# Hyena stage of a hybrid SSD/Hyena/MoE layer: first tap of the short convolution on ScalarE, and the projection halves added ahead of the lane's last remainder

## The reference

```python
u3 = short_conv(p[..., COL_HY:COL_GATE], hy_conv_w, hy_conv_b, rows)   # 3 taps, rows of 64 tokens, zero padding
v, x1, x2 = jnp.split(u3, 3, axis=-1)                                   # 3 x 2048 channels
z2 = x1 * fft_long_conv(v, kf[:, 0], hy_bias[0])
y_hy = x2 * fft_long_conv(z2, kf[:, 1], hy_bias[1])
merged = gates[..., :D] * (y_ssd @ w_ssd_out) + gates[..., D:] * (y_hy @ w_hy_out)
```

## Time and profile before

| | |
|---|---|
| median of 3 runs | 2260.49 us (2258.45 to 2261.85) |
| profiled execution, own time | 2255.41 us |
| its span | 2253.5 us |
| granted TensorE clock, mean | 0.981 |
| TensorE busy, share of span | 95% |
| VectorE / ScalarE / GpSimd busy | 70% / 46% / 5% |
| Hyena lanes 0 to 23 in the span | 734.7 to about 1128 us |

### The profile page before, as it was taken

The page is one execution under the profiler, slowest core; times in us unless marked ns, Lnnn a source line. Parts: engine busy times, 40 slices in busy tenths (PEclk is TensorE's granted clock), DMA queues, the critical chain, the costliest instruction groups (busy, mean ns, idle before and its releaser), DMA issues. The chain is left out here.

```text
span 2253.5 us, 30840 instructions
## 1 busy us (share of the span) xinstructions
PE 2141.1 (95%) x11866; PEld 1734.2 (77%) x11866; DVE 1587.6 (70%) x2195; ACT 1040.5 (46%) x1385; POOL 120.1 (5%) x143
## 2 busy tenths in 40 slices
PE   5999998999999999999999999998899999999997
PEld 2578886546899877777789999986688888778775
DVE  3357787766664678888876445556677777899998
ACT  4243233123654433333443434444655555677776
POOL 2000000000000002020210100000000000000000
PEclk9999999999999999999999999998999999999999
DMA  9954556887576635443434656733588888899995
GB/s 323 366 194 148 189 178 229 302 321 260 176 231 183 178 116 154 133 139 117 136 119 149 173 171 185 242 116 140 161 283 285 272 273 276 311 358 386 364 338 210
DMA packets 314047, 500.60 MB, mean 222 GB/s; under 512 B 16957, under 2 KB 160594, under 8 KB 312752
## 3 DMA queue, kind: packets, MB, share of 16 engines
q1 hardware_dynamic: 308672, 480.80, 64.3%
q0 software_dynamic: 5232, 17.86, 2.4%
HBM read 496.46 MB, written 2.13 MB: 221 GB/s over the span
## 5 line engine op out<-in xcount | busy, mean ns | idle before, releaser
L189 DVE TENSOR_TENSOR w_lo<-raw,w_hi 128x1024 fp32r<-128x1024 f32 x680 | 831.3, 1251 | 373.9 <-ACT w_hi L185 361.9
L185 ACT ACTIVATE w_hi<-raw 128x1024 fp32r<-128x1024 f32 x680 | 707.6, 1058 | 582.0 <-PE bank L197 450.9
L195 PE MATMUL bank<-h,w_hi 128*128 128x256 f32 (+1 forms) x896 | 294.8, 329 | 11.5 <-DVE w_lo L189 5.9
L197 PE MATMUL bank<-h,w_lo 128*128 128x256 f32 (+1 forms) x896 | 290.2, 324 | 0.0
L196 PE MATMUL bank<-h,w_hi 128*128 128x256 f32 (+1 forms) x896 | 290.2, 324 | 0.0
L1624 PE MATMUL bank<-h,w_hi 128*128 128x512 f32 x768 | 280.6, 408 | 4.6 <-DVE w_lo L189 4.6
L1626 PE MATMUL bank<-h,w_lo 128*128 128x256 f32 x768 | 217.9, 284 | 0.0
L195 PEld LDWEIGHTS bank<-h,w_hi 128*128 128x128 f32 x896 | 173.0, 193 | 38.6 <-issue 17.3
L1624 PEld LDWEIGHTS bank<-h,w_hi 128*128 128x128 f32 x768 | 147.3, 192 | 47.5 <-issue 12.3
L197 PEld LDWEIGHTS bank<-h,w_lo 128*128 128x128 f32 x896 | 172.8, 193 | 13.1
L196 PEld LDWEIGHTS bank<-h,w_hi 128*128 128x128 f32 x896 | 173.2, 193 | 12.4 <-issue 0.5
(11 more groups left out here) (498 smaller groups left out, 3684.2 us busy)
## 6 DMA issues: line engine op xcount, KB each, us to landing
raw<-in_w_in SPq DMA_DIRECT2D x240, 512.0 KB, 4.4
raw<-in_ada_w SPq DMA_DIRECT2D x192, 512.0 KB, 6.2
raw<-in_moe_w_gate SPq DMA_DIRECT2D x128, 512.0 KB, 5.2
raw<-in_moe_w_up SPq DMA_DIRECT2D x128, 512.0 KB, 5.6
raw<-in_moe_w_down SPq DMA_DIRECT2D x128, 512.0 KB, 6.0
raw<-in_w_ssd_out SPq DMA_DIRECT2D x32, 512.0 KB, 4.6
raw<-in_w_hy_out SPq DMA_DIRECT2D x32, 512.0 KB, 3.4
raw<-in_w_o SPq DMA_DIRECT2D x32, 512.0 KB, 3.8
```

The source lines that it names most:

```text
L185: act.activation(self.k.w_hi[:, j % HL, :], self.k.raw[:, j % RAW, :], ACT.Copy).then_inc(self.hi_ready, 1)
L189: dve.tensor_tensor(self.k.w_lo[:, j % HL, :], self.k.raw[:, j % RAW, :], self.k.w_hi[:, j % HL, :].bitcast(F32), ALU.subtract).then_inc(s ...
L195: pe.matmul(out, lhs[0], rhs[0], start=start, stop=False)
L197: return pe.matmul(out, lhs[1], rhs[0], start=False, stop=stop)
```

## The change

In lanes b = 1 to 24, for the channels of lane b-1:

- VectorE's `conv` is split. `halves(b-1)`, the two additions L1925, now stands between `split_lo` of q = 2 and of q = 3. The rest stays behind q = 3 (and, where pp is 5, behind `decayed`, `scaled` and `lows`, as before).
- The first tap (two instructions) goes to ScalarE as `first_tap(b-1)`: two `Identity` activations of 128 x 256 with per-channel scale and bias, right behind q3's `split_hi` and so ahead of the side work. It waits for `halves(b-1)`. For the four lanes with b % 6 == 4 the first tap stays on VectorE.
- `conv(b-1)` on VectorE then waits for the first tap and does the four instructions of taps two and three. The waits on `folded` (which keep v and x1 from being overwritten) go to ScalarE with the tap. The counts of `padded` become two per lane.

```diff
-                        pe.wait_ge(s.padded, b - 1)
+                        pe.wait_ge(s.padded, 24 + b - 1)
...
+                def first_tap(b):
+                    i, part, half = b // 6, b % 6 // 2, b % 2
+                    if b % 6 == 4:
+                        return
+                    act.wait_ge(s.summed, b + 1)
+                    if i and part == 0:
+                        act.wait_ge(s.folded, 2 * i - 1)
+                    if i and part == 1:
+                        act.wait_ge(s.folded, 2 * i)
+                    tile = i * 4 + part * KT + 2 * half
+                    for c in range(2):
+                        out = (v, x1, x2)[part][:, 2 * half + c, :].rearrange("p (r n) -> p r n", r=ROWS)
+                        tap = pad[:, c, :].rearrange("p (r n) -> p r n", r=ROWS)[:, :, LEAD:LEAD + GRID_W]
+                        w, bias = VEC_AT["hy_conv_w"] + tile + c, VEC_AT["hy_conv_b"] + tile + c
+                        ins = act.activation(out, tap, ACT.Identity, bias=k.vcol[:, bias:bias + 1],
+                                             scale=k.vcol[:, w:w + 1])
                     ins.then_inc(s.padded, 1)
...
                         st.split_hi(act, 0, 192, HY0 + 4 * b + 3)
+                        if 0 < b < 25:
+                            first_tap(b - 1)
                         if i and pp == 1:
                             keep_spectrum(first)
...
-                def conv(b):
-                    i, part, half = b // 6, b % 6 // 2, b % 2
-                    dve.wait_ge(s.padded, b + 1)
+                def halves(b):
+                    dve.wait_ge(s.padded, 2 * b + 1)
                     for c in range(2):
                         x = rows_of(pad[:, c, :])[:, :, 2:2 + GRID_W]
                         ins = dve.tensor_tensor(x, x, rows_of(k.psum[2 * (b % 2) + c][:, L:2 * L]), ALU.add)
                     ins.then_inc(s.summed, 1)
+
+                def conv(b):
+                    i, part, half = b // 6, b % 6 // 2, b % 2
                     dve.wait_ge(s.summed, b + 1)
-                    if i and part == 0:
-                        dve.wait_ge(s.folded, 2 * i - 1)
-                    if i and part == 1:
-                        dve.wait_ge(s.folded, 2 * i)
-                    if i and part == 2:
-                        dve.wait_ge(s.hi, i)
+                    dve.wait_ge(s.padded, 2 * b + 2)
...
-                    for c in range(2):
-                        own.inc(dve.tensor_scalar(out[c], tap(c, 0), w("hy_conv_w", c), w("hy_conv_b", c),
-                                                  ALU.mult, ALU.add))
+                    if b % 6 == 4:
+                        if i:
+                            dve.wait_ge(s.hi, i)
...
-                        splits(b)
+                        splits(b, range(3))
+                        if 0 < b < 25:
+                            halves(b - 1)
+                        splits(b, range(3, 4))
```

More of the change, by code:

```diff
@@ L1797, in copy_out @@
                                                  bias=k.vcol[:, bias:bias + 1])
+                    ins.then_inc(s.padded, 2 if b < 24 and b % 6 == 4 else 1)
+                def first_tap(b):
[14 more added lines that the diff above has]
+                                             scale=k.vcol[:, w:w + 1])
                     ins.then_inc(s.padded, 1)
@@ L1911, in _, with splits @@
                         first_out()
-                def splits(b):
-                    for q in range(4):
+                def splits(b, some):
+                    for q in some:
                         st.split_lo(dve, 0, 192, HY0 + 4 * b + q)
@@ L1934, in conv @@
                     tile = i * 4 + part * KT + 2 * half
                     dst = (v, x1, x2)[part]
[L1937 to L1944, removed]
-                    for c in range(2):
-                        own.inc(dve.tensor_scalar(out[c], tap(c, 0), w("hy_conv_w", c), w("hy_conv_b", c),
-                                                  ALU.mult, ALU.add))
+                    if b % 6 == 4:
+                        if i:
+                            dve.wait_ge(s.hi, i)
+                        for c in range(2):
+                            at = [VEC_AT[name] + tile + c for name in ("hy_conv_w", "hy_conv_b")]
+                            own.inc(dve.tensor_scalar(rows_of(dst[:, 2 * half + c, :]),
+                                                      rows_of(pad[:, c, :])[:, :, LEAD:LEAD + GRID_W],
+                                                      k.vcol[:, at[0]:at[0] + 1], k.vcol[:, at[1]:at[1] + 1],
+                                                      ALU.mult, ALU.add))
+                        dve.wait_ge(own.sem, own.at())
@@ L1948, in conv @@
                     for t in (1, 2):
                         for c in range(2):
-                            dve.wait_ge(own.sem, own.at(1 if t == 1 else 1 - c))
-                            ins = dve.scalar_tensor_tensor(out=out[c], in0=tap(c, t), scalar=w("hy_conv_w", c, t),
-                                                           in1=out[c], op0=ALU.mult, op1=ALU.add)
+                            out = rows_of(dst[:, 2 * half + c, :])
+                            col = VEC_AT["hy_conv_w"] + tile + c + t * 3 * KT
@@ L1953, in conv @@
+                            if t == 2:
+                                dve.wait_ge(own.sem, own.at(1 - c))
+                            ins = dve.scalar_tensor_tensor(out=out, in0=rows_of(pad[:, c, :])[:, :, LEAD + t:LEAD + t + GRID_W],
+                                                           scalar=k.vcol[:, col:col + 1], in1=out, op0=ALU.mult, op1=ALU.add)
                             if t == 1:
@@ L1957, in merge @@
                 def merge(g):
-                    dve.wait_ge(s.padded, 24 + g + 1)
+                    dve.wait_ge(s.padded, 48 + g + 1)
                     m = k.merged[:, 2 * g + 2:2 * g + 4, :]
```

## The result

| | before | after |
|---|---|---|
| median (6 runs each) | 2261.18 us (2258.45 to 2264.11) | 2274.89 us (2267.74 to 2278.23) |
| ratio, 95% interval | | 1.0062 (1.0043 to 1.0082) |
| profiled execution, own time | 2255.41 us | 2272.36 us |
| its span | 2253.5 us | 2270.6 us |
| lane 0's first matmul to lane 24's | 397.8 us (734.70 to 1132.47) | 413.8 us (737.88 to 1151.63) |

The kernel became slower by 0.6%. Of the 17.1 us between the two profiled spans, 3.2 lie ahead of the Hyena lanes and -2.1 behind them; 16.0 lie inside, where the change is.

A forecast was written before the change was run, and what follows sets the result against it. TensorE was taken to set the pace of the Hyena lanes (385.8 of 396.0 us). Terms -4.5 (filters), +6.6 and +8.1 (delayed spectrum copies) and +5.1 (clock) gave +15.3 us, forecast 2275 us, range 2264 to 2287.

The forecast's parts named there:

- Gain at the filters: Before L1647 in groups 1 to 3: the 1.00 us pause and 0.50 us behind it go, 3 x 1.50 = -4.5 us.
- The tap's cost by itself: On ScalarE, a pair of tap activations takes 0.59 + 0.49 = 1.08 us; lower bound 0.67.
- There is no slack: In mid-`transforms`, s2's weight load starts 0.05 us after the first spectrum copy ends, so delaying the copy stalls TensorE.
- Lane 6i+1: Groups 1 to 3: `keep_spectrum` starts later behind the tap, 3 x 2.2 = +6.6 us; bounds 1.8 and 2.4 each.
- Lane 6i+4: Groups 1 to 3, GpSimd's `fold_v` overlapping: spectrum copy 2.7 us later, 3 x 2.7 = +8.1 us; bounds 1.7 and 3.8 each.
- At nothing: Moved additions (0.75 us, within q3's slab), moved waits on `folded`, and later `keep_turned` and `antis_out` cost no time.
- Clock: TensorE's clock falls behind half of the six new pauses, 3 x 1.7 = +5.1 us; bounds none or 10.2.
- Rival 1: The stalls in `transforms` come but the clock doesn't fall: 2270.7 us; chance 0.17.
- rival 2: The stalls come and the clock falls at each, once or for twice as long: 2281 to 2291 us; chance 0.13.
- Rival 3: VectorE is not late, only the tap's own length shows: +2.0, 2262.5 us, no change to tell; chance 0.10.
- Rival 4: `keep_spectrum` is not late, s2's wait has unseen cover; only the filter gain is left: 2256.0 us; chance 0.08.
- The signs: Changed profile: six new TensorE idle times in `transforms`, some 2.2 and 2.7 us; VectorE's busy time down 13 to 16, ScalarE's up about 23.

The follow-up runs named there:

- the second job: The changed kernel measured again, unchanged, beside the kernel before on one chip: 2277.09 us against 2262.16, ratio 1.0068.
- two-activation kernel: Kernel before plus two unused activations of the tap's size ahead of the spectrum copies in lanes 6i+1 and 6i+4, groups 1 to 3: 2262.53 us, ratio 1.0020.
- the first experiment: Kernel before with only the two additions moved ahead of q3's remainder, all taps still on VectorE: 2255.09 us, ratio 0.9973.
- kernel with earlier additions: Changed kernel with the additions behind q1's remainder instead of q2's in lanes 6i+1 and 6i+4 of groups 1 to 4: 2260.16 us, ratio 0.9997.
- four activations: Kernel before plus four unused activations of the tap's size ahead of the spectrum copies in lanes 6i+1 and 6i+4, groups 1 to 3: 2267.95 us, ratio 1.0047.
- the six taps alone: Changed kernel with only the first taps of convolutions 6, 9, 12, 15, 18 and 21 on ScalarE, the others on VectorE: 2276.68 us, ratio 1.0067.
- the late tap: Changed kernel with ScalarE's first tap behind the four spectrum copies in lanes 6i+1 and 6i+4 of groups 1 to 4: 2256.31 us, ratio 0.9982.

## Why the prediction was right, step by step

The forecast was 2275 us and the measured median is 2274.89. So close a hit owes something to chance. The sum was +15.3 us on a base of 2260.5, or 2275.8, and the two medians differ by 13.7 (14.9 in the second job, where the same kernel gave 2277.09); the base came out 0.7 higher, and two terms were off in opposite ways.

- *The bound and the chains.* Right. Only the filter pause hung on the convolution; the 1.54 and 2.6 us pauses kept their length.
- *Gain at the filters, -4.5 us.* Measured 1.00 + 0.37 us each, -4.1. The pause went; of the 0.50 behind it 0.13 stayed (1.19 against 1.06 us in group 4).
- *The tap's cost by itself, 1.08 us.* 1.10 in the trace. What the Trainium skill, "ScalarE: Activation LUTs", section "Rules for kernel authors", says against additions and multiplications on ScalarE (VectorE up to about three times faster per element, in bf16) did not set the price in this float32 kernel: by its factor, an estimate, the six places would have cost 0.8 us more each, and they didn't. What counts is where the tap stands.
- *"There is no slack".* Nearly: 0.13 us by the two-activation kernel.
- *Lane 6i+1, 3 x 2.2.* Measured 2.25 us in lane 7, where the clock held, and 2.41 there in the second profile, where TensorE came to `transforms` 0.15 us earlier in the lane.
- *Lane 6i+4, 3 x 2.7.* Measured 2.28: the term was too large by 0.4 us each. The third remainder ended 2.42 us behind the start of `transforms`, where I had 2.56; the additions and the tap overlap by 0.1 more than I had; and I had left out the load's lead, which I had taken off in lane 6i+1. The upper bound, additions slowed by GpSimd, is excluded by the lane 10 rows (0.74 us beside `fold_v`). That agrees with the Trainium skill, "GPSIMD Engine Reference", section "Key points", which names instructions with two SBUF inputs: the remainder (two) took 1.62, the additions (one in PSUM) their usual time. The section names those in a 2-port mode as well; the first tap, with one SBUF tile, took 3.71 us a pair beside GpSimd, and no run here shows its mode.
- *At nothing.* Shown by the first experiment: `halves` ahead costs nothing, also in group 0. The fourteen other taps cost nothing either.
- *Clock, three falls of 1.7, +5.1.* In the changed kernel's profile four falls of about 1.8, +7.1. The fall at lane 24's head didn't come, outside the length of lanes given above. The count was a guess with a wide bound, and it is the term that made up for the one above. With the stalls of group 1 taken for all groups, 6.75 + 6.84 - 4.1 + 7.1 = 16.6 for the lanes, where 16.0 were measured.
- *The rivals.* Rival 1 (no fall) lost to the profile, and so did rival 2 (a fall at each): four of six. Rival 3 (VectorE not late) is what the kernel with earlier additions makes true in lane 6i+4, and there the cost is indeed the tap's length. Rival 4 fell with the two-activation kernel: the copies have 0.13 us of cover, not 0.75.
- *The signs.* As forecast, but for three sizes: the new idle times were 2.0 to 2.2 us, not 2.2 and 2.7; VectorE's work fell by 17.5 us, not 13 to 16 (first taps 23.7 less, taps two and three 7.2 more, remainders 2.1 less); ScalarE's rose by 21.1, not 23.

Left open: what decides whether the clock falls. Behind seventeen pauses of 0.6 to 1.7 us inside `transforms` (two and four activations, earlier additions) it never fell, behind eighteen of 2.0 to 2.7 us (the changed kernel in two profiles, the six taps alone) twelve times; but behind the 1.54 us at the head of lane 6 it fell in all ten profiles that have this pause, and at the heads of lanes 12, 18 and 24, with the same 1.54 us, in eight, seven and six of them.

## What to carry to other kernels

An engine with half of its time free is no free place. Before an instruction is moved there, look at what stands behind it in that engine's program and who waits for that; here fourteen of twenty moved instructions cost nothing and six cost 2.3 us each, with a fall of the clock at four of them, and putting them behind the four copies gave it all back. If a moved instruction waits for a third engine, its own length need not be the larger part of the price (here 0.85 of 2.25 us): add what stands in that engine's queue ahead of what it waits for.

## What the runs showed of the hardware

A fall of the clock that goes away doesn't give all of its time back, since TensorE then runs into the next wait. Where the clock held at the head of lane 12, 18 or 24, a new pause of 0.2 to 1.0 us stood at the head of the `transforms` a lane later, ended by VectorE's `taps`: 0.86 us in the kernel with the additions ahead (lane 19), 0.4 with the late tap, 0.98 with two activations (lane 13), 0.19 in the changed kernel (lane 25). In all eleven profiles the pause stands there where the clock held, and nowhere else. So equal work differs by some microseconds between kernels by where the clock falls, while single pieces repeat: a `transforms` of groups 1 to 3 without a stall inside took 6.56 or 6.67 us in every profile, where the medians of the kernel before scatter by several us.
